# Gated-linear heads of a hybrid block: tanh swishes, late squares, and low parts of weight tiles made by VectorE instead of GpSimd

## The chip, the cores and the metric

One core of a Trainium2 chip runs the whole kernel as one program. The metric is the device time of that core in microseconds. Three runs before the change took 5358.28, 5361.36 and 5364.64 us; the median is 5361.36.

## The reference

The reference is one layer: a normalised input is projected by one large matrix; a state-space branch (SSD), a gated linear branch (HGRN2) and gates are mixed and projected; then follows a mixture of experts over product keys. Sequence 512, width 2048, all in float32. The change touches the gated linear branch alone (16 heads, key and value width 128):

```
qh = silu(hq);  f = lb + (1 - lb) * sigmoid(hf);  kh = 1 - f;  log_f = log(f);  vh = hi
per chunk:  bcum = cumsum(log_f)
            scores[t,s] = sum_k q[t,k] k[s,k] exp(bcum[t,k] - bcum[s,k])      (s <= t)
            o = scores @ v + (q * exp(bcum)) @ state
            state = exp(b_end) * state + (k * exp(b_end - bcum))^T @ v
o = rms(o) * hg_norm_w * silu(hg);   y_hg = o
```

`hq`, `hf`, `hi`, `hg` are the projections of the normalised input `h` (512 x 2048) with the head's columns of four 2048 x 2048 matrices. `rms(o)` is `o * rsqrt(mean(o^2) + 1e-6)` over the head's 128 values.

## The kernel before

**Stages.** `program` runs stages one after the other: norm, SSD, the gated heads (`hg_stage`, L726, from 798.5 us to about 1827 us of the profiled execution), two mix stages, an output projection, and the experts. Channels lie on the partitions and the 512 tokens on the free axis.

**A product in float32.** Each weight tile (128 output channels, 128 x 2048 numbers in SBUF) is split in two rounded parts: `high` is a rounded copy made by ScalarE (`split_high`, L148), `low = raw - high` is made by GpSimd (`split_low`, L155). `product` (L168) adds for each of 16 steps three matmuls of 128x128 by 128x512: high by h_high, high by h_low, low by h_high; 48 matmuls a tile, 24 in each half of a tile. The ring `Ring` has two slots each of `raw`, `high` and `low`. SP loads raw tile n when the low part of tile n-2 is done (`load_tile`, L127: one 1 MB transfer). ScalarE makes the high part of tile n when TensorE has used tile n-2 and the load has landed. `ring.used` counts the tiles that TensorE has finished.

**A head.** Four tiles, in the order f, q, v (hi), g (hg); n = 4u + s is tile s of head u. The accumulators `acc[0]` and `acc[1]` alternate; each is free for its next tile when what was in it has been read (`acc_read`). The computation on head p = u - 1 is placed by TensorE between the halves of head u's tiles:

- `turn` (L871): four transposes each of v and of the decayed keys `lev[:, L8]`, into `ps_v` and `ps_k`.
- `part_a` (L879, L880): for one chunk c of 128 tokens, seven level products and one for the diagonal, into `ps_lev`. It needs the preceding block to have been read (`a_read`).
- `part_b` (L889 to L894): for chunk c the value product, for c > 0 the product with the state, for c < 3 the new state's contribution. It needs `probs` of the chunk and, for c > 0, the state.
- after the first half of tile 3, the sum of squares over the head's channels with a matrix of ones (L928).

**VectorE** (in the order of its queue, for u in the loop): copies v_tok and k_tok from PSUM; `take_probs(p, 0)` and `(p, 1)` (a masked product L995 and a sum over levels L997); `take_f(u)`: sigmoid of f by an addition, a reciprocal (L971) and a scaling, then k = 1 - f, and four scans of the logarithms (L979); `next_state` and `take_probs` for chunks 0 to 3; the swish of q: `1 + exp(-x)` (L986), reciprocal (L987), multiply (L988); `exponents(u)`: differences for seven levels in halves (L1017, L1018) and two more rows, with `next_state(p, 2)` among them; the copy of v out of its accumulator (L1064); `weigh(u)`: 14 multiplies (L1029, L1030), copies, `qe`, the copy of four columns `k_end` (L1036) and the decayed keys (L1037); then `o_norm` of head p in two operations (L1073 with the root, L1075 with the gate); the swish of g like that of q.

**ScalarE**: high part of tile 1; exp of -f; Ln of f; high part of tile 2; exp of -q; high part of tile 3; one exponential of nine level rows (L844, 4608 columns, after all differences); squares of the output (L847, after `part_b` of chunk 3); high part of the next head's tile 0; Ln and Exp for the inverse root (L851, L853); exp of -g. All functions are in one set of activation tables, loaded once in this stage.

**Order around the change.** There is no planner: each engine runs its own queue in the written order with semaphore waits. The head loop runs over u = 1..15 with a first body (projection only) and a last one (computation only) outside of it. SP stores o_norm of head u - 2 after the four loads of head u.

Of the kernel before, what the change touches and what calls it, by code (L numbers as in the profile page):

```python
# [27 lines left out]
EXP_LN_SET = "natural_log_exp_and_others"  # L28

P = 128  # L30
# [695 lines left out]
def hg_stage(nc, dram, ring, h, const, y_out, following):  # L726
# [8 lines left out]
    with ExitStack() as ctx:  # L735
# [7 lines left out]
        norm_w = sb("norm_w", [P, 1])  # L743
        f = sb("f", [P, T])
# [28 lines left out]
        f_exp, q_exp, g_exp, f_ready, f_log, b_ready = (  # L773
            sem(n) for n in ("f_exp", "q_exp", "g_exp", "f_ready", "f_log", "b_ready"))
# [4 lines left out]
        lev_ready = sem("lev_ready")  # L779
        a_done = sem("a_done")  # L780
# [4 lines left out]
        squared, summed, rooted = sem("squared"), sem("summed"), sem("rooted")  # L785
        o_ready = sem("o_ready")
        o_stored = sem("o_stored")
        act_done, vec_done = sem("act_done"), sem("vec_done")
        block = ctx.enter_context(nc.Block())

        @block.sync
        def _(sp):
# [10 lines left out]
            for s in range(HG_TILES):  # L803
                load_tile(sp, ring, s % 2, dram["w_hg"][HG_TILES + s], HG_TILES + s)
            with sp.Fori(2, H) as u:
# [3 lines left out]
                store(u - 2)  # L809
            load_ahead(sp, ring, H * HG_TILES, following)  # L810
            store(H - 2)
            store(H - 1)
            sp.wait_ge(o_stored, 16 + 16 * H)

        @block.gpsimd
        def _(pool):
            split_low_all(nc, pool, ring, H * HG_TILES)

        @block.scalar
        def _(act):  # L820
# [5 lines left out]
            def body(u, proj, comp):  # L826
                p = u - 1
                for s in range(HG_TILES):
                    n = HG_TILES * u + s
                    if proj:  # L830
                        split_high(nc, act, ring, (s + 1) % 2, n + 1, 2 * u + (s + 1) // 2)
                    if s == 0 and proj:
                        act.wait_ge(ring.used, ring.base + n + 3)
                        act.wait_ge(lev_ready, u + 1)
                        nc.scalar.activation(f[:], acc[0][:], ACT.Exp, scale=-1.0).then_inc(f_exp, 1)
                        act.wait_ge(f_ready, u + 1)
                        nc.scalar.activation(b[:], f[:], ACT.Ln).then_inc(f_log, 1)
                    if s == 1 and proj:
                        act.wait_ge(ring.used, ring.base + n + 3)
                        nc.scalar.activation(sg[:], acc[1][:], ACT.Exp, scale=-1.0).then_inc(q_exp, 1)  # L840
                    if s == 2:
                        if proj:
                            act.wait_ge(lev_diff, u + 1)
                            nc.scalar.activation(lev[:, 0:LK], lev[:, 0:LK], ACT.Exp).then_inc(lev_exp, 1)  # L844
                        if comp:
                            act.wait_ge(b_done, NC * p + NC)
                            nc.scalar.activation(o_sq[:], ps_o[:], ACT.Square).then_inc(squared, 1)  # L847
                    if s == 3:
                        if comp:
                            act.wait_ge(summed, p + 1)  # L850
                            chain.after(nc.scalar.activation(rstd[:], ps_k[:], ACT.Ln, bias=const["eps"],  # L851
                                                             scale=1.0 / P))
                            nc.scalar.activation(rstd[:], rstd[:], ACT.Exp, scale=-0.5).then_inc(rooted, 1)  # L853
                        if proj:
# [5 lines left out]
            with act.Fori(1, H) as u:  # L860
                chain.enter(u - 1, 1)
                body(u, True, True)
# [1209 lines left out]
```

## Time and profile before

| | value |
|---|---|
| median of three runs | 5361.36 us |
| profiled execution, its time | 5372.8 us |
| its span | 5370.8 us |
| mean granted TensorE clock | 0.963 |
| TensorE matmuls, busy | 4992.5 us, 93% |
| VectorE, busy | 3406.7 us, 63% |
| ScalarE, busy | 1451.5 us, 27% |
| GpSimd, busy | 2024.3 us, 38% |

"Busy" is the sum of the times in which an engine's instructions ran, and "span" goes from the first instruction to the last. The granted clock is the share of 2.4 GHz that TensorE was given: 0.5 is 1.2 GHz. Consecutive matmuls overlap in these records, so that the distance from one start to the next (the pitch) is what a matmul costs in a stream; a matmul of 512 columns lasts 0.39 us but starts some 0.23 us after the one before. The same holds to a lesser degree for VectorE and ScalarE.

### The profile page before, as it was taken

How to read it: one execution, taken by the hardware profiler on the slowest of the kernel's cores; microseconds unless marked ns; L12 is line 12 of the kernel's file. 1: busy time of each engine (PE TensorE's matmuls, PEld its weight loads, DVE VectorE, ACT ScalarE, POOL GpSimd, SP SyncE). 2: the span in 40 equal slices, each digit the busy share in tenths (PEclk: the TensorE clock that was granted, in tenths of full speed). 3: DMA queues.
4: the chain of work that ended last, by engine and by line, in shares of the span. 5: the costliest groups of instructions: out<-in, count | busy, mean ns of one | idle time of the engine just before them, and what ended most of it. 6: DMA issues, size and time to landing. Idle time of an engine off the chain costs nothing. (4 is left out here: it accounts for less than half of the span.)

```text
span 5370.8 us, 69570 instructions
## 1 busy us (share of the span) xinstructions
PE 4992.5 (93%) x25836; PEld 4479.2 (83%) x25836; DVE 3406.7 (63%) x4674; ACT 1451.5 (27%) x1170; POOL 2024.3 (38%) x624
## 2 busy tenths in 40 slices
PE   6999979999889899999869989999999799999997
PEld 5877857777777688788658989999999799999997
DVE  3566657888888500100127879998444588888886
ACT  2233222222222222211222324343222222222222
POOL 2333313333333244344334445556989411111111
PEclk7999989999999899999989999999999899999999
DMA  2222212121122223333323337777877888888884
GB/s 76 87 86 86 82 53 75 67 81 67 66 70 80 84 105 107 143 117 117 147 98 108 115 132 278 257 263 281 304 298 298 314 300 300 299 301 300 300 300 159
DMA packets 230889, 913.26 MB, mean 170 GB/s; under 512 B 18353, under 2 KB 100913, under 8 KB 152625
## 3 DMA queue, kind: packets, MB, share of 16 engines
q1 hardware_dynamic: 193968, 644.12, 34.6%
q0 software_dynamic: 36864, 268.45, 13.4%
q8 instruction: 29, 0.48, 0.0%
q14 instruction: 28, 0.22, 0.0%
HBM read 837.00 MB, written 75.50 MB: 170 GB/s over the span
## 5 line engine op out<-in xcount | busy, mean ns | idle before, releaser
L157 POOL TENSOR_TENSOR ring_low<-ring_raw,ring_high 128x2048 fp32r<-128x2048 f32 x337 | 1648.3, 4893 | 2068.9 <-ACT ring_high L152 2068.2
L175 PE MATMUL rt_acc<-h_high,ring_high 128*128 128x384 f32 (+1 forms) x2304 | 793.7, 345 | 24.5 <-POOL ring_low L157 21.5
L176 PE MATMUL rt_acc<-h_low,ring_high 128*128 128x384 f32 (+1 forms) x2304 | 785.9, 341 | 0.0
L177 PE MATMUL rt_acc<-h_high,ring_low 128*128 128x384 f32 (+1 forms) x2304 | 785.8, 341 | 0.0
L152 ACT ACTIVATE ring_high<-ring_raw 128x2048 fp32r<-128x2048 f32 x337 | 645.0, 1914 | 390.3 <-PE out_acc L177 125.1
L1695 DVE CUSTOM_DVE_ANT_0 sb_rt_rows<-sb_rt_rows,sb_rt_h_tok 128x2048 f32<-128x2048 f32 x128 | 339.4, 2651 | 277.7 <-DMA sb_rt_rows<-u_rows,row_of 274.5
L175 PE MATMUL hg_acc<-h_high,ring_high 128*128 128x512 f32 x1024 | 429.2, 419 | 59.8 <-POOL ring_low L157 50.5
L1319 POOL DMA_INDIRECT sb_op_rows<-v_tiles,row_of x128 | 122.6, 958 | 948.0 <-DVE sb_op_total L1860 922.5
L175 PEld LDWEIGHTS rt_acc<-h_high,ring_high 128*128 128x128 f32 x2304 | 433.9, 188 | 41.2 <-POOL ring_low L157 17.0
L176 PEld LDWEIGHTS rt_acc<-h_low,ring_high 128*128 128x128 f32 x2304 | 433.9, 188 | 10.0
L177 PEld LDWEIGHTS rt_acc<-h_high,ring_low 128*128 128x128 f32 x2304 | 433.5, 188 | 10.3
L176 PE MATMUL hg_acc<-h_low,ring_high 128*128 128x512 f32 x1024 | 410.3, 401 | 0.0
L177 PE MATMUL hg_acc<-h_high,ring_low 128*128 128x512 f32 x1024 | 410.2, 401 | 0.0
L1833 PE MATMUL op_out<-sb_op_w_high,ring_high 128*128 128x384 f32 x1024 | 343.3, 335 | 26.6 <-DVE sb_op_w_low L1876 26.6
L1833 PE MATMUL op_out<-sb_op_w_high,sb_op_more_high 128*128 128x384 f32 x1024 | 343.4, 335 | 7.2 <-DVE sb_op_more_low L1866 7.2
L1835 PE MATMUL op_out<-sb_op_w_high,sb_op_more_low 128*128 128x384 f32 x1024 | 343.2, 335 | 0.0
L1834 PE MATMUL op_out<-sb_op_w_low,sb_op_more_high 128*128 128x384 f32 x1024 | 343.1, 335 | 0.0
L1834 PE MATMUL op_out<-sb_op_w_low,ring_high 128*128 128x384 f32 x1024 | 343.0, 335 | 0.0
L1835 PE MATMUL op_out<-sb_op_w_high,ring_low 128*128 128x384 f32 x1024 | 343.0, 335 | 0.0
L175 PE MATMUL ssd_acc<-h_high,ring_high 128*128 128x512 f32 x768 | 304.3, 396 | 0.0
L1896 DVE TENSOR_TENSOR x_mid_back<-x_mid_back,op_out 128x384 f32<-128x384 f32 x512 | 270.2, 548 | 49.9 <-PE op_out L1835 49.9
L1860 DVE SCALAR_TENSOR_TENSOR sb_op_total<-sb_op_rows,own_weight,sb_op_total 128x2048 f32<-128x2048 f32 x128 | 300.1, 2345 | 0.0
(294 smaller groups left out, 10031.0 us busy)
## 6 DMA issues: line engine op xcount, KB each, us to landing
ring_raw<-u_tiles SPq DMA_DIRECT2D x128, 1024.0 KB, 5.1
ring_raw<-v_tiles SPq DMA_DIRECT2D x128, 1024.0 KB, 6.0
ring_raw<-w_hg SPq DMA_DIRECT2D x64, 1024.0 KB, 4.8
ring_raw<-w_ssd SPq DMA_DIRECT2D x48, 1024.0 KB, 4.8
ring_raw<-w_mix_s SPq DMA_DIRECT2D x32, 1024.0 KB, 4.8
ring_raw<-w_mix_h SPq DMA_DIRECT2D x32, 1024.0 KB, 4.9
gelu<-sb_rt_gelu SPq DMA_DIRECT2D x128, 192.0 KB, 4.9
gates<-sb_rt_table SPq DMA_DIRECT2D x12, 2048.0 KB, 8.4
```

The lines of the kernel that those rows point to most:

```text
L152: nc.scalar.activation(ring.high[:, slot], ring.raw[:, slot], ACT.Copy).then_inc(ring.high_ready, 1)
L157: nc.gpsimd.tensor_tensor(ring.low[:, slot], ring.raw[:, slot], ring.high[:, slot].bitcast(F32), ALU.subtract).then_inc(ring.low_ready, 1)
L175: nc.tensor.matmul(out, high[:, m], x_high[:, k, tokens], start=(k == 0), stop=False, skip_group_check=True)
L176: nc.tensor.matmul(out, high[:, m], x_low[:, k, tokens], start=False, stop=False, skip_group_check=True)
L177: last = nc.tensor.matmul(out, low[:, m], x_high[:, k, tokens], start=False, stop=(k == KT - 1), skip_group_check=True)
L1319: return pool.indirect_dma_start(rows[0:OWN, slot], None, table, bass.IndirectOffsetOnAxis(ap=row_of[0:OWN, k:k + 1], axis=0))
L1695: vec.tensor_tensor_reduce(rows[0:OWN, slot], rows[0:OWN, slot], h_tok[0:OWN], 1.0, 0.0, ALU.mult, ALU.add, dot[0:OWN, slot:slot + 1]).the ...
L1833: nc.tensor.matmul(o, v_high[s][:, m], w_high[:, buf, j], start=(j == 0), stop=False)
L1834: nc.tensor.matmul(o, v_high[s][:, m], w_low[:, buf, j], start=False, stop=False)
L1835: last = nc.tensor.matmul(o, v_low[s][:, m], w_high[:, buf, j], start=False, stop=(j == GROUP - 1))
L1860: vec.scalar_tensor_tensor(total[0:OWN], rows[0:OWN, slot], weight[0:OWN, ds(k, 1)], total[0:OWN], ALU.mult, ALU.add).then_inc(summed, 1)
L1896: vec.tensor_tensor(x, x, ps_out[d][:, 0:REST], ALU.add).then_inc(out_added, 1)
```

## The change

It keeps the mathematics of the heads and changes who does what, and when:

- **Late squares.** The sum of squares of head p goes to TensorE's slot after the first half of tile 0 of the head after next; the root and the last multiply (now a factor in `ps_k`) follow there. Before that `o_norm` receives `ps_o * norm_w * og` (`o_weighed`). The loop has a third part, `fin`, for head u - 2, and runs over u = 2..15 with two bodies ahead of it and two behind.
- **Low parts.** VectorE makes all four low parts of a head at fixed places of its queue (`low(u, s)`). GpSimd has no instruction in this stage.
- **Order of TensorE.** The computation moves ahead by about half a tile: `part_a` and `part_b` end after the second half of tile 2, and both halves of tile 3 run without an interruption. `turn(ps_k, ...)` moves behind the second half of tile 0.
- **Order of VectorE and ScalarE.** `take_f` comes ahead of `k_tok` and `take_probs(p, 1)`; `exponents` ahead of `take_probs(p, 3)`; v is read after `weigh`. The exponential of the level rows is cut in two (five rows and four), and `k_end` is copied by ScalarE.
- **SP.** Stores stand after the second load of a head, for head u - 3.

The core of the diff (unchanged lines of the moved parts left out):

```diff
+                nc.scalar.preload_act_table_set(EXP_LN_SET)
+                if proj:
+                    next_high(0)
+                if fin:
+                    act.wait_ge(summed, e + 1)
+                    chain.after(nc.scalar.activation(rstd[:], ps_k[:], ACT.Ln, bias=eps4[:], scale=1.0 / P))
+                    nc.scalar.activation(ps_k[:], rstd[:], ACT.Exp, scale=-0.5).then_inc(rooted, 1)
+                if proj:
+                    act.wait_ge(ring.used, ring.base + HG_TILES * u + 3)
+                    act.wait_ge(lev_ready, u + 1)
+                    nc.scalar.activation(f[:], acc[0][:], ACT.Exp, scale=-1.0).then_inc(f_exp, 1)
+                    next_high(1)
+                    act.wait_ge(f_ready, u + 1)
+                    nc.scalar.activation(b[:], f[:], ACT.Ln).then_inc(f_log, 1)
+                    nc.scalar.preload_act_table_set(EXP_TANH_SET)
+                    act.wait_ge(ring.used, ring.base + HG_TILES * u + 4)
+                    nc.scalar.activation(sg[:], acc[1][:], ACT.Tanh, scale=0.5).then_inc(q_tanh, 1)
+                    next_high(2)
+                    act.wait_ge(lev_diff, 2 * u + 1)
+                    nc.scalar.activation(lev[:, 0:FIRST_EXP], lev[:, 0:FIRST_EXP], ACT.Exp).then_inc(lev_exp, 1)
+                    act.wait_ge(lev_diff, 2 * u + 2)
+                    nc.scalar.activation(lev[:, FIRST_EXP:LK], lev[:, FIRST_EXP:LK], ACT.Exp).then_inc(lev_exp, 1)
+                    act.wait_ge(lev_exp, 2 * u + 2)
+                    if comp:
+                        act.wait_ge(state_ready, (NC - 1) * p + (NC - 1))
+                    nc.scalar.activation(k_end[:], ..., ACT.Copy).then_inc(k_end_ready, 1)
+                if comp:
+                    act.wait_ge(b_done, NC * p + NC)
+                    nc.scalar.activation(o_sq[:], ps_o[:], ACT.Square).then_inc(squared, 1)
+                if proj:
+                    next_high(3)
+                    act.wait_ge(ring.used, ring.base + HG_TILES * u + 6)
+                    act.wait_ge(acc_read, HG_TILES * u + 4)
+                    nc.scalar.activation(sg[:], acc[1][:], ACT.Tanh, scale=0.5).then_inc(g_tanh, 1)
...
+                half(0, 0)
+                if fin:
+                    pe.wait_ge(squared, e + 1)
+                    nc.tensor.matmul(ps_k[:], const["ones"], o_sq[:], start=True, stop=True).then_inc(summed, 1)
+                if comp:
+                    pe.wait_ge(lev_ready, p + 2)
+                    pe.wait_ge(acc_read, HG_TILES * p + 5)
+                    turn(ps_v, v)
+                    part_a(p, 0)
+                half(0, 1)
+                if comp:
+                    pe.wait_ge(o_ready, p + 1)
+                    turn(ps_k, lev[:, L8])
+                    part_a(p, 1)
+                half(1, 0)
+                if comp:
+                    part_b(p, 0)
+                    part_a(p, 2)
+                half(1, 1)
+                if comp:
+                    part_b(p, 1)
+                    part_a(p, 3)
+                half(2, 0)
+                if comp:
+                    part_b(p, 2)
+                half(2, 1)
+                if comp:
+                    part_b(p, 3)
+                half(3, 0)
+                half(3, 1)
...
+            def low(u, s):
+                slot, n = s % 2, HG_TILES * u + s
+                dve.wait_ge(ring.high_ready, ring.base + n + 1)
+                vec.tensor_tensor(ring.low[:, slot], ring.raw[:, slot], ring.high[:, slot].bitcast(F32),
+                                  ALU.subtract).then_inc(ring.low_ready, 1)
...
+            def twice_swish(dst, src, tanh_done, value, taken):
+                dve.wait_ge(tanh_done, value)
+                vec.scalar_tensor_tensor(dst[:], sg[:], 1.0, src[:], ALU.add, ALU.mult).then_inc(acc_read, 1)
+                dve.wait_ge(acc_read, taken)
...
             def weigh(u, p, comp):
-                dve.wait_ge(lev_exp, u + 1)
                 for l, w in enumerate(HALVES):
+                    if l == 0:
+                        dve.wait_ge(lev_exp, 2 * u + 1)
+                    if l == FIRST_EXP:
+                        dve.wait_ge(lev_exp, 2 * u + 2)
+                        low(u, 4)
...
+                if proj:
+                    low(u, 1)
                 if comp:
                     dve.wait_ge(turned, 2 * p + 1)
                     vec.tensor_copy(v_tok[:].rearrange("p c v -> p (c v)"), ps_v[:]).then_inc(turned_read, 1)
+                if fin:
+                    dve.wait_ge(rooted, e + 1)
+                    dve.wait_ge(o_weighed, e + 2)
+                    vec.tensor_tensor(o_norm[:], o_norm[:], ps_k[:], ALU.mult).then_inc(o_ready, 1)
+                if comp:
+                    take_probs(p, 0)
+                if proj:
+                    take_f(u)
+                if comp:
                     dve.wait_ge(turned, 2 * p + 2)
                     vec.tensor_copy(k_tok[:].rearrange("p c v -> p (c v)"), ps_k[:]).then_inc(turned_read, 1)
                     take_probs(p, 1)
                 if proj:
+                    low(u, 2)
+                    sum_logs(u)
                 if comp:
                     next_state(p, 0)
                     take_probs(p, 2)
                     next_state(p, 1)
+                if proj:
+                    twice_swish(q, acc[1], q_tanh, u + 1, n + 4)
+                    low(u, 3)
+                    if comp:
+                        dve.wait_ge(a_done, NC * p + NC)
+                    exponents(u)
+                if comp:
                     take_probs(p, 3)
                     next_state(p, 2)
                 if proj:
                     weigh(u, p, comp)
                     dve.wait_ge(ring.used, ring.base + n + 5)
                     vec.tensor_copy(v[:], acc[0][:]).then_inc(acc_read, 1)
+                    dve.wait_ge(acc_read, n + 5)
                 if comp:
+                    dve.wait_ge(squared, p + 1)
                     dve.wait_ge(o_stored, 16 * p + 16)
+                    if fin:
+                        dve.wait_ge(o_ready, e + 2)
+                    vec.scalar_tensor_tensor(o_norm[:], ps_o[:], norm_w[:, 0:1], og[:],
+                                             ALU.mult, ALU.mult).then_inc(o_weighed, 1)
+                    dve.wait_ge(o_weighed, p + 2)
                 if proj:
+                    twice_swish(og, acc[1], g_tanh, u + 1, n + 6)
```

`next_high(s)` is `split_high` of tile s + 1 of the head. `sum_logs` is the part of `take_f` with the scans.

## Rows read from the trace of the kernel before

**Rows 1.** Stretches: us, busy time of each engine, granted clock, DMA share, GB/s.

```profile
900.00:1780.00 880.00, 800.00 (x3988) 668.32 (x3987) 741.71 (x903) 213.98 (x168) 313.68 (x56) 0.96 0.20 71
300.00:700.00 400.00, 395.15 (x1946) 318.33 (x1945) 261.20 (x326) 118.15 (x125) 137.00 (x31) 1.00 0.24 85
```

**Rows 2.** Waits of TensorE, 850 to 1795 us: total, times, longest.

```profile
PE hg_acc L175 <- POOL ring_low L157: 49.1, 14, 3.5
PE hg_ps_k L928 <- ACT sb_hg_o_sq L847: 33.1, 15, 2.2
```

**Rows 3.** TensorE in order of time, one head: start, us, line [idle before].

```profile
1229.59 0.79 PE L175 MATMUL hg_acc<-h_high,ring_high 128*128 128x512 f32 x1 [3.50 <-POOL ring_low L157]
...
1236.69 0.60 PE L871 MATMUL hg_ps_v<-c_ident,sb_hg_v 128*128 128x128 f32 x4
...
1244.82 1.72 PE L879 MATMUL hg_ps_lev<-sb_hg_lev 128*128 128x128 f32 x14
...
1246.52 0.48 PE L175 MATMUL hg_acc<-h_high,ring_high 128*128 128x512 f32 x1
...
1252.10 0.39 PE L889 MATMUL hg_ps_o<-sb_hg_probs,sb_hg_v_tok 128*128 128x128 f32 x2
...
1254.25 0.48 PE L175 MATMUL hg_acc<-h_high,ring_high 128*128 128x512 f32 x1
...
1279.54 0.39 PE L177 MATMUL hg_acc<-h_high,ring_low 128*128 128x512 f32 x1
1282.13 1.12 PE L928 MATMUL hg_ps_k<-sb_hg_o_sq,c_ones 128*128 128x512 f32 x2 [2.20 <-ACT sb_hg_o_sq L847]
...
1292.22 0.79 PE L175 MATMUL hg_acc<-h_high,ring_high 128*128 128x512 f32 x1 [3.48 <-POOL ring_low L157]
```

**Rows 4.** Groups of the stage: busy us, mean ns; the last: ns min/median/max, starts.

```profile
L997 DVE TENSOR_REDUCE sb_hg_probs<-sb_hg_masked 128x128 f32<-128x1024 f32 x64 | 128.0, 2000 | 2.2
L987 DVE RECIPROCAL sb_hg_sg<-sb_hg_sg 128x512 f32<-128x512 f32 x32 | 107.3, 3353 | 1.1
L995 DVE TENSOR_TENSOR sb_hg_masked<-hg_ps_lev,sb_hg_mask 128x1024 f32<-128x1024 f32 x64 | 78.0, 1219 | 64.8 <-PE hg_ps_lev L880 64.8
...
L152 ACT ACTIVATE ring_high<-ring_raw 128x2048 fp32r<-128x2048 f32 x64 | 121.8, 1903 | 0.0
L844 ACT ACTIVATE sb_hg_lev<-sb_hg_lev 128x4608 f32<-128x4608 f32 x16 | 64.8, 4052 | 237.4 <-DVE sb_hg_lev L1021 237.4
...
L157 POOL TENSOR_TENSOR ring_low<-ring_raw,ring_high x64: 4574/4632/8132, 805.2 to 1789.1; 128x2048 fp32r<-128x2048 f32 x64
```

**Rows 5.** Three lines by instance: ns min/median/max, first and last start.

```profile
L1036 DVE COPY sb_hg_k_end<-sb_hg_lev x16: 4495/4506/4516, 849.9 to 1792.8; 128x4 f32<-128x4 f32 x16
...
L1075 DVE TENSOR_TENSOR sb_hg_o_norm<-sb_hg_o_norm,sb_hg_og x16: 691/4058/4083, 914.8 to 1826.3; 128x512 f32<-128x512 f32 x16
...
L1866 DVE TENSOR_TENSOR ring_low<-ring_raw,ring_high x63: 2227/2286/2293, 4238.0 to 5285.1; 128x2048 fp32r<-128x2048 f32 x63
```

**Rows 6.** VectorE in order of time, same head.

```profile
1249.96 0.42 DVE L968 TENSOR_SCALAR sb_hg_sg<-sb_hg_f 128x512 f32<-128x512 f32 x1
...
1254.53 0.43 DVE L975 TENSOR_SCALAR sb_hg_k<-sb_hg_f 128x512 f32<-128x512 f32 x1
1255.26 1.37 DVE L979 TENSOR_TENSOR_SCAN sb_hg_b<-c_ones,sb_hg_b 128x128 f32<-128x128 f32 x4 [0.30 <-ACT sb_hg_b L837]
...
1271.53 0.42 DVE L1017 TENSOR_TENSOR sb_hg_lev<-sb_hg_b 128x256 f32<-128x256 f32 x1
...
1276.49 0.42 DVE L1019 COPY sb_hg_lev<-sb_hg_b 128x512 f32<-128x512 f32 x1
```

**Rows 7.** ScalarE in order of time, a table switch of the earlier stage.

```profile
519.69 1.28 ACT L436 ACT_TABLE_LOAD   x1
520.99 0.69 ACT L436 ACTIVATE sb_ssd_rstd<-ssd_ps_decay,c_eps 128x512 f32<-128x512 f32 x1
```

**Rows 8.** One matmul of each step, whole stage: ns min/median/max, first and last start.

```profile
L175 PE MATMUL hg_acc<-h_high,ring_high x1024: 387/389/798, 798.8 to 1793.0; 128*128 128x512 f32 x171
```

More of the change, by code:

```diff
@@ L28 @@
 EXP_LN_SET = "natural_log_exp_and_others"
+EXP_TANH_SET = "exp_and_others"
 P = 128
@@ L801, in store @@
                 sp.dma_start(one(y_out[ds(p, 1)]), o_norm[:]).then_inc(o_stored, 16)
-            for s in range(HG_TILES):
-                load_tile(sp, ring, s % 2, dram["w_hg"][HG_TILES + s], HG_TILES + s)
-            with sp.Fori(2, H) as u:
+            for n in range(HG_TILES, 3 * HG_TILES):
+                load_tile(sp, ring, n % 2, dram["w_hg"][n], n)
+            with sp.Fori(3, H) as u:
                 for s in range(HG_TILES):
@@ L808, in _ @@
                     load_tile(sp, ring, s % 2, one(dram["w_hg"][ds(n, 1)]), n)
-                store(u - 2)
+                    if s == 1:
+                        store(u - 3)
             load_ahead(sp, ring, H * HG_TILES, following)
-            store(H - 2)
-            store(H - 1)
+            for p in range(H - 3, H):
+                store(p)
             sp.wait_ge(o_stored, 16 + 16 * H)
-        @block.gpsimd
-        def _(pool):
-            split_low_all(nc, pool, ring, H * HG_TILES)
         @block.scalar
@@ L824, in _, with body, next_high @@
             nc.scalar.activation(lb_in[:], lb_in[:], ACT.Exp).then_inc(lb_step, 1)
-            def body(u, proj, comp):
-                p = u - 1
-                for s in range(HG_TILES):
+            def body(u, proj, comp, fin):
+                p, e = u - 1, u - 2
+                def next_high(s):
                     n = HG_TILES * u + s
[L830 to L854, printed above, removed]
-                            act.wait_ge(ring.used, ring.base + n + 3)
-                            act.wait_ge(acc_read, HG_TILES * u + 4)
-                            nc.scalar.activation(sg[:], acc[1][:], ACT.Exp, scale=-1.0).then_inc(g_exp, 1)
@@ new lines, in body @@
+                if proj:
[16 more added lines that the diff above has]
+                        act.wait_ge(state_ready, (NC - 1) * p + (NC - 1))
+                    nc.scalar.activation(k_end[:], lev[:, L7].rearrange("p (c t) -> p c t", c=NC)[:, :, CH - 1],
+                                         ACT.Copy).then_inc(k_end_ready, 1)
@@ L866, in _ @@
+            body(1, True, True, False)
+            with act.Fori(2, H) as u:
+                chain.enter(u - 2, 1)
+                body(u, True, True, True)
+            chain.leave(H - 2)
+            body(H, False, True, True)
+            body(H + 1, False, False, True)
         @block.tensor
@@ L895, in part_b, with body, half @@
                 last.then_inc(b_done, 1)
[L897 to L899 removed]
+            def body(u, proj, comp, fin):
+                p, e = u - 1, u - 2
+                def half(s, i):
                     n = HG_TILES * u + s
[L902 to L937 removed]
@@ L939, in _ @@
-            body(0, True, False)
-            with pe.Fori(1, H) as u:
-                body(u, True, True)
-            body(H, False, True)
+                    if not proj:
+                        return
+                    if i == 0:
+                        pe.wait_ge(ring.low_ready, ring.base + n + 1)
+                        pe.wait_ge(acc_read, n + 1)
+                    last = product(nc, acc[s % 2][:], ring.high[:, s % 2], ring.low[:, s % 2], h[0], h[1],
+                                   range(i * KT // 2, (i + 1) * KT // 2))
@@ L944, in _ @@
+                half(2, 1)
[3 more added lines that the diff above has]
+                half(3, 1)
+            body(0, True, False, False)
+            body(1, True, True, False)
+            with pe.Fori(2, H) as u:
+                body(u, True, True, True)
+            body(H, False, True, True)
+            body(H + 1, False, False, True)
         @block.vector
```

129 lines of the change are left out of this document (39 added, 90 removed).

## The prediction

> **What bounds the kernel now.** I read the busy shares, then the stage in stretches, then who waits, then TensorE and VectorE in order of time. In the steady heads TensorE is busy 800.0 of 880 us at a granted clock of 0.96, VectorE 741.7; the 400 us of the earlier stage show 395.2 of 400 at 1.00 [rows 1]. So TensorE's stream is the floor, and about a tenth of it is lost. The list of waits gives two losses, 14 and 15 times: 3.5 us for `ring_low` and 2.2 us for the squares [rows 2]. The timeline shows a third: the first half tile of a head takes 1236.69 - 1229.59 = 7.10 us after the 3.50 us wait, while the one that ends the stretch from 1246.52 to 1252.10 takes 5.58; the first matmul after the wait lasts 0.79 us, where one before the squares lasts 0.39: half the granted clock (1.2 of 2.4 GHz), then the full one [rows 3]. One head takes 1292.22 - 1229.59 = 62.63 us.
>
> Without the losses a head is: a first half of 5.55, then 1236.69 to the end of the sixth later interruption, 1279.54 + 0.23 = 1279.77, 43.08 us, then 0.56 for the sum over squares (half of the row's 1.12, whose two records overlap like all here) and the last half of 5.55: **54.7 us** [rows 3]. The parts I need: both transposes and the first level block 2.57 (from 1236.69 to the half that ends at 1244.82, so began at 1239.26), a level block 1.70 (1244.82 to 1246.52), first value product with the third level block 2.15 (1252.10 to 1254.25). The remaining small work in 43.08, less six halves of 5.55 and 2.57 + 1.70 + 2.15, is 3.4: about 2.4, 0.6 and 0.4.
>
> GpSimd takes 4.6 us for a low part where nothing disturbs it, up to 8.1 [rows 4]. Why it is late: its operand waits for ScalarE's high part, and that stands in ScalarE's queue behind the 4.05 us exponential of all nine level rows, which waits for VectorE. VectorE in turn carries two reciprocals of 3.35 us for swishes [rows 4], a 4.5 us copy of 128x4 and an o_norm multiply of 4.06 us whose shortest instance is 0.69 [rows 5]: I read nearly all of both as VectorE held off while GpSimd is on a low part.
>
> **The change, part by part, per head.** VectorE's own sum: two reciprocals and their additions go (2 x 3.35, and 0.43 each by the row at 1249.96 for the same shape), -7.6; the k_end copy goes to ScalarE, -4.5; the multiply falls from 4.06 to 0.69, -3.4; four low parts come, 4 x 2.29 [rows 5], +9.2. Net about -6.3 from 741.7 / 880 x 62.7 = 52.8 us: 46.5. It stays under 54.7. GpSimd's 4.6 us and more per tile leave the path; the wait for the low part of the next head's first tile goes if VectorE gives it in time.
>
> That is a matter of order, so I lay it out. Zero is TensorE's start on a head. TensorE with the new order: half to 5.5, sum 6.1, turn v and level block 0 to 8.3, half to 13.8, turn k and block 1 to 15.9, half to 21.5, value product 0 and block 2 to 23.6, half to 29.2, product 1 and block 3 to 31.6, half to 37.2, product 2 37.8, half to 43.3, product 3 43.7, two halves to 54.7.
>
> VectorE starts its long run when the f tile is done: 13.8, ScalarE's exponential 0.6 and two hand-overs of 0.1 to 0.3, so 14.8. The row at 1249.96 to the one at 1254.53 is 4.57 [rows 6]: k starts at 19.3. k 0.4, k_tok 0.6: 20.3. Block 1's masked product 1.2 (21.5) and sum 1.95: 23.5. Low part 2 at a pitch of 2.2: 25.7. Four scans 1.3: 27.0. State 0.2, block 2's probabilities 3.2, state 0.3: 30.7. The q swish 0.75, 31.4. Low part 3 must wait for ScalarE: q's tile ends at 29.2, tanh, then the high part of 1.90 [rows 4] to 31.9: so 31.9 to 34.2. Level differences: 1276.49 - 1271.53 = 4.96 less one state update of 0.26 = 4.7 [rows 6], two more operations about 1.0: 39.9. Probabilities 3: 43.0. State: 43.3. TensorE wants these at 43.3 for product 3. **That is a tie**, the tightest place; the masked product of block 1, read at 21.5, stands against block 2 at 21.95, and that of block 2 at 28.5 against block 3 at 29.9.
>
> From 43.3: ten weighings at 0.335, 46.7 (their exponentials, 4.05 x 5/9 = 2.3 from 37.6 and 1.9 from 39.9, are done by 41.8). Low part 4: ScalarE copies k_end after the last state, squares after product 3 (43.9 to 44.5), high part to 46.4; low 46.7 to 48.9, wanted at 54.7. Four weighings, four copies and products: 52.1; v read from its bank at 52.8, which TensorE wants at 54.7: 1.9 spare. The og swish waits for the last tile and ends at 56.4, 1.7 into the next head.
>
> Next head: ScalarE's tanh ends at 0.9, table load 1.28 [rows 7], high part to 4.1; low part 1 at 4.1 to 6.4, wanted at 15.9. The squares are a head old, so the 2.2 us wait goes; Ln and Exp to 7.6, o_norm 8.6, probabilities 0 to 11.8, and VectorE idles until 14.8. The gap takes up all late work of the loop turn. The transfers: a slot is loaded when VectorE's low part frees it (6.4, 25.7, 34.2, 48.9) and its high part is wanted 8 us later or more, against some 5 us that a tile took; SP's store now stands after the second load and waits for an o_norm written 25 us before. Hidden.
>
> The two table switches cost 1.28 each in the row, with the next activation 0.02 later [rows 7]. The Trainium skill (ScalarE: Activation LUTs, What ACT_TABLE_LOAD costs) gives 1.28 plus a drain, 2.66 in all, and its advice to group functions by set speaks against switching twice a head. With its price low part 1 would end at 7.8 and probabilities 0 at 13.2: still inside the idle gap, so the sum would differ only in the tail, by 1.4 us.
>
> **The sum.** Before, TensorE's projections run from 798.8 to 1793.0 + 0.7: 994.9 us [rows 8]. After: head 0 has no computing beside it: 192 matmuls at 0.227 (5.45 / 24, a half less its first 0.1) = 43.5 and 1.8 for the cold start; then 15 heads of 54.7 plus 0.4, taken for loop turns and for the tie at product 3, the side the estimates err to: 15 x 55.1 = 826.5. 871.8 in all: 123 saved. Tail: before 33.3 us from the last projection to the last o_norm at 1826.3 + 0.7 [rows 5, 8], which includes waiting for the k_end copy and two reciprocals; with these gone, four probabilities at 3.2, hand-overs, one root and one multiply make about 25: 8 saved, bounds 4 and 12 (the two reciprocals alone, and all the k_end and multiply waiting besides). Together 131. The profiled execution took 5372.8 (span 5370.8): it would be 5242. The median of the runs is 11.4 lower than the profiled one; the same saving gives **5230 us**.
>
> Unseen prices: a tanh of 128x512, bounded by the exponentials of the shape at 0.60 and 0.63; ScalarE's output into PSUM, never in these rows, between 0 and 1 us more than the 0.63 into SBUF, and inside the idle gap; the scalar_tensor_tensor of a swish, 0.69 to 0.75 by the multiply of the shape. The low part on VectorE is taken at 2.29; from above GpSimd's longest, 8.13 [rows 4]. The row of 2.29 is nearest: the same form on the same tiles, 63 times; below it lies its own shortest, 2.23.
>
> **Rivals.**
> 1. VectorE's run sets the pace at product 3. It is tied, so each microsecond too little in my run from 14.8 to 43.3 (some twenty operations and six hand-overs) is a microsecond of TensorE's idle time per head. For 1 to 3 us: 15 to 45 us given back, 5245 to 5275; I take 5260. For: no slack at all. Against: pitches are from this stage, some taken under GpSimd's disturbance.
> 2. The same wait grows past 3 us, and the clock falls as behind the 3.5 us wait, at least 1.6 us more (1229.59 to 1236.69 against 5.55). Head 59 to 61: saving 131 - 15 x 5 = 55: 5305.
> 3. Slower: a low part costs on VectorE what it cost disturbed on GpSimd, say 6.4, the middle of 4.63 and 8.13 [rows 4], because the tiles' memory and not the engine sets its pace while loads and ScalarE use it. Two lie in the run before product 3: +8.2, and +2 for the clock (1.6 and rounding): a head of 64.9, 15 x 64.9 + 45.3 = 1018.8 against 994.9, less the tail's 8: 5377. It decides from a low part of about 5.8. Against it: none of 63 over 2.293 with loads running [rows 5].
> 4. No effect: TensorE finds a new wait of equal size in each head, such as turn k behind o_ready (8.6 against 13.8, 5 us spare; it must be 13 late): 5361.
>
> **Chances.** Forecast 0.6, rival 1 0.22, rival 2 0.08, rival 3 0.06, rival 4 0.04. The forecast's own width is 5222 (no friction, tail 12) to 5245; the range, 5220 to 5285, takes rival 1 whole. A measurement of this kernel tells 0.2%, 11 us, from no change: faster 0.9, same 0.04, slower 0.06.
>
> **What would show it.** Stage: last projection near 1671; granted clock 1.00 in the steady heads, TensorE idle under 1 us a head. VectorE: low parts at 2.29 with ScalarE's high part as releaser at low parts 1 and 3 alone; the longest idle time before the f addition, about 3 us; no 4 us instance of the o_norm multiply; 46 us busy a head. TensorE's wait, if any, at product 3. If instead waits stand at block 2 or at the first half of a head, my order of VectorE's work is wrong; if the clock is below 0.98 with no waits above 2 us, the floor is.

## The result, and the profile after

The changed kernel takes **5236.4 us** (median of four runs, 5234.6 to 5238.1) against 5363.0 us before; the ratio is 0.9757, 95% interval 0.9745 to 0.9768. Forecast: 5230, range 5220 to 5285. The profiled execution went from 5372.8 to 5234.9 us. 137.9 us are more than the 126.6 of the medians because the profiled execution of before lay 9.8 above its median, that of after 1.5 below.

Stretches of the changed kernel (columns as in [rows 1]): the steady heads, and the tail behind the last projection. In the first TensorE is busy without a gap at the full clock, where [rows 1] had 800 of 880 us at 0.96; GpSimd did nothing.

```profile
900.00:1640.00 740.00, 740.00 (x3863) 627.83 (x3862) 606.31 (x846) 251.42 (x217) 0.00 (x0) 1.00 0.23 80
...
1669.10:1691.70 22.60, 14.45 (x97) 11.40 (x95) 17.10 (x17) 6.34 (x8) 0.00 (x0) 0.94 0.03 12
```

The row of the first matmul of each step, and those of the low part and the late o_norm multiply (ns min/median/max, first and last start). The first answers to [rows 8]: 868.2 us between the first and the last start, against 994.2. The second is [rows 5]'s price for a low part; the third has no instance near the 4 us of before.

```profile
L176 PE MATMUL hg_acc<-h_high,ring_high x1024: 387/389/767, 800.2 to 1668.4; 128*128 128x512 f32 x171
...
L990 DVE TENSOR_TENSOR ring_low<-ring_raw,ring_high x64: 2278/2292/2297, 808.4 to 1660.9; 128x2048 fp32r<-128x2048 f32 x64
...
L1082 DVE TENSOR_TENSOR sb_hg_o_norm<-sb_hg_o_norm,hg_ps_k x16: 686/687/689, 908.1 to 1691.0; 128x512 f32<-128x512 f32 x16
```

The list of waits between 850 and 1668 us holds no line of TensorE; both of [rows 2] are gone. VectorE waits for ScalarE's high part twice a head and for f's exponential once:

```profile
DVE ring_low L990 <- ACT ring_high L153: 46.3, 30, 2.5
DVE sb_hg_sg L996 <- ACT sb_hg_f L845: 43.7, 15, 2.9
```

VectorE in order of time, the head whose first matmul starts at 1229.7 (1235.16, where the sum of squares starts, less a half of 5.45). To be seen: the gap of 2.92 before the f gate, the 0.59 before low part 3, and the state that is done at 1272.80 + 0.35.

```profile
1233.86 2.29 DVE L990 TENSOR_TENSOR ring_low<-ring_raw,ring_high 128x2048 fp32r<-128x2048 f32 x1 [2.46 <-ACT ring_high L153]
...
1244.61 0.43 DVE L996 TENSOR_SCALAR sb_hg_sg<-sb_hg_f 128x512 f32<-128x512 f32 x1 [2.92 <-ACT sb_hg_f L845]
...
1261.79 2.29 DVE L990 TENSOR_TENSOR ring_low<-ring_raw,ring_high 128x2048 fp32r<-128x2048 f32 x1 [0.59 <-ACT ring_high L153]
...
1270.88 2.01 DVE L1024 TENSOR_REDUCE sb_hg_probs<-sb_hg_masked 128x128 f32<-128x1024 f32 x1
1272.80 0.35 DVE L1032 SCALAR_TENSOR_TENSOR sb_hg_state<-sb_hg_state,sb_hg_k_end,hg_ps_state 128x128 f32<-128x128 f32 x1
...
1281.95 0.69 DVE L1110 COPY sb_hg_v<-hg_acc 128x512 f32<-128x512 f32 x1
```

TensorE's product 3 of the same head starts 0.1 us behind that state. Its first matmul needs only the probabilities, whose sum over levels ended at 1270.88 + 2.01 = 1272.89; the matmul that reads the state is the second:

```profile
1273.26 0.38 PE L903 MATMUL hg_ps_o<-sb_hg_probs,sb_hg_v_tok 128*128 128x128 f32 x2
1273.48 0.39 PE L906 MATMUL hg_ps_o<-sb_hg_qe,sb_hg_state 128*128 128x128 f32 x2
```

### The profile page after: what moved, and what is told of

The parts are those of the page before. It is cut to its first block and busy times, and to the rows that moved or that the text cites. A ratio compares the mean times of both kernels' runs of the same rounds, so it can differ in the third digit from the quotient of the medians.

```text
span 5232.2 us, 69516 instructions
## 1 busy us (share of the span) xinstructions
PE 4945.5 (95%) x25836; PEld 4450.6 (85%) x25836; DVE 3275.9 (63%) x4660; ACT 1503.2 (29%) x1236; POOL 1661.0 (32%) x560
## 5 line engine op out<-in xcount | busy, mean ns | idle before, releaser
L158 POOL TENSOR_TENSOR ring_low<-ring_raw,ring_high 128x2048 fp32r<-128x2048 f32 x273 | 1294.9, 4744 | 2295.7 <-ACT ring_high L153 2295.0
L176 PE MATMUL hg_acc<-h_high,ring_high 128*128 128x512 f32 x1024 | 408.4, 399 | 9.2 <-DVEq L968 9.2
L178 PE MATMUL ssd_acc<-h_high,ring_low 128*128 128x512 f32 x768 | 300.3, 391 | 0.0
```

The costliest lines, as they stand in the source:

```text
L158: nc.gpsimd.tensor_tensor(ring.low[:, slot], ring.raw[:, slot], ring.high[:, slot].bitcast(F32), ALU.subtract).then_inc(ring.low_ready, 1)
L176: nc.tensor.matmul(out, high[:, m], x_high[:, k, tokens], start=(k == 0), stop=False, skip_group_check=True)
L178: last = nc.tensor.matmul(out, low[:, m], x_high[:, k, tokens], start=False, stop=(k == KT - 1), skip_group_check=True)
```

## The experiments

"Stage" below is the distance between the first and the last start of the projections' first matmul, in the profiled execution: 994.2 before, 868.2 after. I compare by it because one later stage, the experts' routing, took 1378 to 1383 us in some executions and 1408 to 1413 in others, whichever of these kernels ran; the medians of whole runs carry that 30 us.

| | median, us | stage, us | one head, us | TensorE's waits in the stage, us a head |
|---|---|---|---|---|
| before | 5363 to 5368 | 994.2 | 62.6 or 63.7 | low part 3.5, squares 2.2 |
| after | 5236.4 | 868.2 | 54.9 | none |
| e1 low parts on GpSimd | 5296.5 | 930.4 | 59.0 | product 3 1.7, k_tok 1.1, block 2 0.4 |
| e2 tanh alone | 5261.6 | 893.4 | 56.6 | low part 1.4 |
| e3 VectorE low parts alone | 5307.4 | 935.4 | 58.6 or 60.2 | squares 2.2, state 0.7 |
| e4 exp swishes | 5287.6 | 918.0 | 58.0 | product 3 2.8; v's bank 2.2 once |
| e5 one operation in the run | 5240.8 | 875.1 | 55.4 | product 3 0.2 |
| e6 four operations | 5282.5 | 914.1 | 57.5 or 59.0 | product 3 2.3 |
| e7 two behind product 3 | 5237.7 | 868.7 | 54.9 | none |
| e8 sum back in tile 3 | 5223.2 | 870.5 | 55.0 | none |
| e9 idle work on GpSimd | 5322.5 | 958.3 | 59.2 or 60.8 | product 3 2.8, block 2 0.4; v's bank 7.7 once |
| e10 two switches in the gap | 5239.6 | 868.4 | 54.9 | none |
| e11 two switches in the run | 5285.1 | 917.5 | 57.35 or 58.9 | product 3 2.1; v's bank 1.9 once |
| e12 five behind product 3 | 5239.6 | 898.8 | 56.8 | v's bank 1.6 |

"One head" is the distance between two f gates (`sb_hg_sg<-sb_hg_f` on VectorE) once the loop runs steadily. Where two lengths stand, the longer head has a stretch at half the clock (before the change both have one, the longer head a longer one). "Once" is a wait at the start of head 1, ahead of the steady heads.

**What carries the gain.** e1 takes the low parts back to GpSimd:

```diff
             def low(u, s):
-                ... (wait and subtraction)
+                return
+        @block.gpsimd
+        def _(pool):
+            split_low_all(nc, pool, ring, H * HG_TILES)
```

> The changed kernel with one part undone: GpSimd makes the four low parts of a head again, VectorE makes none. Theory A (order and tanh carry the gain; the low parts on VectorE carry nothing of it): TensorE's stream of 54.9 us a head stays the bound, GpSimd's 4.6 us ends before each tile is wanted, time within 0.3% of the changed kernel, 5236 us. Theory B (VectorE and GpSimd hold each other off, so the low parts had to move): copies and tensor_scalar operations of VectorE wait 2 to 4 us again in the run from f to product 3 and TensorE waits there, 2 to 5 us a head: 5265 to 5310 us.

Measured: 62 us more stage. My theory A fell, B's figures held. The result of the low part is never late in the steady heads (no wait for `ring_low` behind 850 us). VectorE has less to do than in the changed kernel, 578.1 us busy in 800 against 606.3 in 740, 42.6 us a head against 45.0, and is late all the same, because its own work is held off: of the fourteen level differences the first now takes 4.85 us, started 0.04 behind GpSimd's low part, and f's scaling 2.75 where it took 0.55. The sum of eight stretches of 100 us from 900 us on, then VectorE, then GpSimd in this kernel:

```profile
sum 800.00, PE 756.24 PEld 630.89 DVE 578.11 ACT 251.25 POOL 296.32; mean PE 94.53 PEld 78.86 DVE 72.26 ACT 31.41 POOL 37.04
```

```profile
1233.94 4.85 DVE L1043 TENSOR_TENSOR sb_hg_lev<-sb_hg_b 128x256 f32<-128x256 f32 x1 [0.90 <-DVE sb_hg_q L1016]
...
1277.67 2.75 DVE L1000 TENSOR_SCALAR sb_hg_f<-sb_hg_sg,sb_hg_lb 128x512 f32<-128x512 f32 x1 [0.19 <-DVE sb_hg_sg L999]
```

```profile
1233.90 4.60 POOL L158 TENSOR_TENSOR ring_low<-ring_raw,ring_high 128x2048 fp32r<-128x2048 f32 x1 [12.81 <-ACT ring_high L153]
1250.48 7.99 POOL L158 TENSOR_TENSOR ring_low<-ring_raw,ring_high 128x2048 fp32r<-128x2048 f32 x1 [11.98 <-ACT ring_high L153]
...
1275.51 4.62 POOL L158 TENSOR_TENSOR ring_low<-ring_raw,ring_high 128x2048 fp32r<-128x2048 f32 x1 [8.07 <-ACT ring_high L153]
```

The Trainium skill (SBUF — State Buffer, Who interferes with whom) says that the two engines share one pair of ports under an exclusive lock, that a VectorE instruction with two SBUF inputs contends there with a GpSimd instruction that reads SBUF, and that the order of issue decides which of them blocks the other. These rows agree: the difference that starts at 1233.94 ends at 1238.79, 0.29 behind the end of GpSimd's low part (1233.90 + 4.60), f's scaling, started at 1277.67, ends 0.29 behind another (1275.51 + 4.62), and GpSimd's 4.6 becomes 8 at 1250.48, in the middle of VectorE's weighings.

e9 tests that alone: all as after, and GpSimd subtracts constants that nobody reads. The core of its edit:

```diff
...
+                pool.wait_ge(ring.high_ready, i + (ring.base + 2))
+                for j in range(2):
+                    nc.gpsimd.tensor_tensor(pool_spare[:, j], mask[:], mask[:], ALU.subtract)
```

> The changed kernel, VectorE still making the low parts, with idle work on GpSimd beside it: at each high part it subtracts two constant tiles of 128x1024 into a spare tile, twice, about 4.6 us in all, which nobody waits for. Theory B (the two engines hold each other off on their common way to SBUF): VectorE's low parts and the first operation behind them last up to 4.6 us longer, the run to product 3 grows by 2.3 to 7 us and TensorE waits there: stage 35 to 120 us longer. Rival (GpSimd's work costs VectorE nothing; what made the kernel with low parts on GpSimd slower was waiting for the results alone): under 5 us.

Measured: 90 us more, inside B's range; 10 of them fall once, before the steady heads, where TensorE waits 7.7 us for v's copy. In a steady head two level differences of 2.12 and 2.11 us stand in a row, each behind one of GpSimd's two operations; low part 3 itself kept 2.29, against the expectation. The rival is out, since nobody waits for GpSimd's results here:

```profile
1248.57 2.29 DVE L1001 TENSOR_TENSOR ring_low<-ring_raw,ring_high 128x2048 fp32r<-128x2048 f32 x1 [0.45 <-ACT ring_high L153]
1250.78 2.12 DVE L1053 TENSOR_TENSOR sb_hg_lev<-sb_hg_b 128x256 f32<-128x256 f32 x1
1252.82 2.11 DVE L1054 TENSOR_TENSOR sb_hg_lev<-sb_hg_b 128x256 f32<-128x256 f32 x1
```

e2 is the kernel before with the tanh swishes only (norm weight halved, 4 eps, four switches a head):

```diff
-                chain.after(vec.tensor_scalar(sg[:], sg[:], 1.0, None, ALU.add))
-                chain.after(vec.reciprocal(sg[:], sg[:]))
-                vec.tensor_tensor(dst[:], src[:], sg[:], ALU.mult).then_inc(acc_read, 1)
+                vec.scalar_tensor_tensor(dst[:], sg[:], 1.0, src[:], ALU.add, ALU.mult).then_inc(acc_read, 1)
```

> The kernel before with one part of the change: both swishes by tanh (four table switches a head), all else in the old order, low parts on GpSimd. Theory A: the level differences end 5.1 us earlier, so the exponential ends near 46.8 us into a head of 62.6 and not 52, the squares are ready before TensorE asks, and the low part of the next head's first tile is late by 0 to 1.2 us only: head 55 to 56.5, saving 90 to 115 us, 5250 to 5275 us. Theory B: GpSimd's low part is still the last thing at the head's end, disturbed to 6 to 8 us, and the 3.5 us wait stays while only the wait for the squares goes: head near 60, saving 35 to 45 us, 5320 us.

Measured: 100.8 of the stage's 126.0 us, a head of 56.6 us, so theory A. The squares' wait is gone and one for GpSimd is left (14 instances, 1.4 us each); one low part of that kernel, at 1235.34, lasts 8.17 us:

```profile
PE hg_acc L176 <- POOL ring_low L158: 18.9, 14, 1.4
```

e3 is the other part alone, `low(u, s)` at the start, behind `take_f`, behind the q swish and after ten weighings:

```diff
-            split_low_all(nc, pool, ring, H * HG_TILES)
...
+                    low(u, 1)
...
+                    low(u, 2)
...
+                    low(u, 3)
...
+                    low(u, 4)
```

> The kernel before with the other part alone: VectorE makes the low parts (tile 1 at the head's start, 2 behind the f gate, 3 behind the q swish, 4 behind ten weighings), swishes by reciprocals, old order. Both theories: k_end's copy falls from 4.5 to under 0.3 us and every o_norm multiply to 0.7 us, since GpSimd is idle. Theory A (the level run to the squares is what counts): 4.4 us more in that run, TensorE's wait for the squares grows from 2.2 to about 6.6 us and eats what the vanished 3.5 us wait gives: 5345 to 5400 us, no gain. Theory B (the mutual holding off is what cost): several us less on VectorE in each head, time 5270 to 5310 us.

Measured: 58.8 us off the stage. k_end's copy and the o_norm multiply fell as both theories said, below; A was wrong on the time. The run from the scans to the last level difference went from 1255.26 to 1276.83 + 0.68 before ([rows 6] for its start) to 1227.40 to 1250.93 here: 22.3 to 23.5 us, though two low parts of 2.2 us were put in. Of the 3.2 us that they did not cost, 2.7 had been in it already: a wait of 1.44 us for TensorE's block 3 and an addition (L986) that took 1.72 and not 0.43 behind GpSimd. VectorE of the kernel before, then two groups of e3:

```profile
1262.46 1.23 DVE L995 TENSOR_TENSOR sb_hg_masked<-hg_ps_lev,sb_hg_mask 128x1024 f32<-128x1024 f32 x1 [1.44 <-PE hg_ps_lev L880]
...
1265.67 1.72 DVE L986 TENSOR_SCALAR sb_hg_sg<-sb_hg_sg 128x512 f32<-128x512 f32 x1
...
1276.83 0.68 DVE L1021 TENSOR_TENSOR sb_hg_lev<-sb_hg_b 128x512 f32<-128x512 f32 x1
```

```profile
L1040 DVE COPY sb_hg_k_end<-sb_hg_lev x16: 158/162/164, 849.0 to 1735.5; 128x4 f32<-128x4 f32 x16
...
L1083 DVE TENSOR_TENSOR sb_hg_o_norm<-sb_hg_o_norm,sb_hg_og x16: 692/692/694, 908.3 to 1764.6; 128x512 f32<-128x512 f32 x16
```

So neither part is enough, and the two overlap: 100.8 and 58.8 alone, 126.0 with both and the new order. The new order does not pay by itself. With the tanh swishes and GpSimd's low parts, the new order and what goes with it give a stage of 930.4 (e1), the old order 893.4 (e2): 37 us worse. In e1 f's scaling and the first level difference, both in the run to product 3, stand where GpSimd is on a low part. With VectorE's low parts and the old swishes the new order is 17 us better (e4 918.0, e3 935.4). The 62 us of e1 are thus the price of GpSimd's low parts in this order, not in general. Both parts in the old order were not run, so the order's own share of the 126.0 is open. e4 is the changed kernel with the old swishes and no switches:

```diff
-                vec.scalar_tensor_tensor(dst[:], sg[:], 1.0, src[:], ALU.add, ALU.mult).then_inc(acc_read, 1)
+                chain.after(vec.tensor_scalar(sg[:], sg[:], 1.0, None, ALU.add))
+                chain.after(vec.reciprocal(sg[:], sg[:]))
+                vec.tensor_tensor(dst[:], src[:], sg[:], ALU.mult).then_inc(acc_read, 1)
```

> The changed kernel with its swishes by exp, addition and reciprocal again (no table switches then), new order, low parts on VectorE. Theory A (product 3 is tied to VectorE's run): the q swish adds 3.8 us of which 0.5 lay in the wait for low part 3: TensorE waits 3.2 us at product 3, plus up to 2.4 us of half clock behind it: 15 x 3.2 to 5.6 = 48 to 84 us slower, 5285 to 5320 us. Rival (there is slack in the order that the layout misses): under 15 us slower.

Measured: 49.8 us: 3.06 in each steady head (57.98 against 54.92) and 4.0 once before them; the wait at product 3 is there in all 15 heads, 2.8 us each, and the stretches from 900 to 1700 us all show a granted clock of 1.00.

```profile
PE hg_ps_o L901 <- DVE sb_hg_probs L1023: 41.7, 15, 2.8
```

e8 puts the sum of squares back to tile 3 (`half(3, 0)`, sum, `half(3, 1)`).

```diff
-                if fin:
-                    pe.wait_ge(squared, e + 1)
-                    nc.tensor.matmul(ps_k[:], const["ones"], o_sq[:], ...).then_inc(summed, 1)
...
                 half(3, 0)
+                if comp:
+                    pe.wait_ge(squared, p + 1)
+                    nc.tensor.matmul(ps_k[:], const["ones"], o_sq[:], ...).then_inc(summed, 1)
                 half(3, 1)
```

> The changed kernel with TensorE's sum of squares back behind the first half of tile 3, where it was before the change; root and last multiply stay late. Theory A (the squares are ready 5 us before TensorE asks there, since the exponentials end early; their lateness is not what pays): no wait, stage within 2 us of the changed kernel. Rival (the late place is what removes the 2.2 us wait): 1 to 2.2 us a head, 15 to 33 us longer.

Measured: 2.3 us more stage, 0.09 a head, and no wait. TensorE asks at 1280.30 for squares that ScalarE began at 1275.00. The late place is not what removed the 2.2 us wait.

```profile
1275.00 0.60 ACT L864 ACTIVATE sb_hg_o_sq<-hg_ps_o 128x512 f32<-128x512 f32 x1 [0.50 <-PE hg_ps_o L906]
```

**How tight the order is.** e5, e6 and e7, e12 add operations of 0.7 us to VectorE: one and four ahead of `take_probs(p, 3)`, two and five behind `weigh`. That of e5:

```diff
+                    for _ in range(1): 
+                        chain.after(vec.tensor_tensor(spare[:], b[:], b[:], ALU.add))
```

> The changed kernel with one operation more on VectorE ahead of the probabilities of chunk 3 (the addition of two 128x512 tiles into a spare one, waited for: about 0.72 us), in each of 15 heads. Theory A (product 3 tied to VectorE's run, 0.1 us spare in the trace of the changed kernel): TensorE waits 0.6 us at product 3 in each head, stage 9 us longer. Rival (at least 1 us of slack there): no wait, stage unchanged within 1 us.

> The same with four such operations, 2.9 us. Theory A: a wait of 2.8 us at product 3 in each head, stage 42 us longer with the clock kept. Rival 2 of the prediction (the clock falls behind the wait): 1.6 us or more on top, stage 65 us or more longer. Slack theory: under 30 us.

> The changed kernel with two such operations, 1.4 us, behind the weighing and ahead of v's copy, past product 3. Theory A (2.0 us spare there): no wait on TensorE, stage unchanged within 2 us. Rival (VectorE's whole queue is the bound, every microsecond on it counts): 15 x 1.4 = 21 us longer.

> The changed kernel with five operations of 0.72 us, 3.6 us, ahead of v's copy, where the trace shows 2.0 us spare. Theory A: v is read 1.6 us after TensorE wants the accumulator, TensorE waits there at the head's first half: 15 x 1.6 = 24 us longer. If the two ops run had shown no cost for another reason than spare time, this one shows none either.

Measured: +6.9 and +45.9 us for 0.7 and 2.9 us in the run; +0.5 and +30.6 for 1.4 and 3.6 us behind it. A head of e5 takes 55.40 us, 0.48 more for 0.73 added; ten heads of e6 take 57.5, 2.57 more for 2.91, and five about 59.0, with a stretch at half the clock behind the wait: theory A, with the 1.5 us of rival 2 in a third of the heads. A head of e12 takes 56.77, 1.85 more for 3.6. Between the first and second pair lies the whole statement: some 0.3 us spare before product 3, 1.8 to 2.0 behind it. The wait of e12 is 24.6 us over 15 heads, 1.64 each (one of 2.84, the others 1.55), where 1.6 was expected:

```profile
PE hg_acc L176 <- DVE sb_hg_v L1113: 24.6, 15, 2.8
```

**The price of a table switch.** e10 puts two more at the head's start, e11 two between q's tanh and the next high part. That of e11:

```diff
+                    nc.scalar.preload_act_table_set(EXP_LN_SET)
+                    nc.scalar.preload_act_table_set(EXP_TANH_SET)
                     next_high(2)
```

> The changed kernel with two table switches more at the head's start (three in a row for one). Priced by the rows of the trace, 1.28 us each: the first high part ends 2.6 us later, inside VectorE's idle gap of 2.9 us before the f gate: no wait, stage within 3 us. A price of 2.66 us each, estimate by the Trainium skill (ScalarE: Activation LUTs, What ACT_TABLE_LOAD costs): 5.3 us later, the f gate starts 1.3 to 2.4 us late, and the tie at product 3 turns it into 15 to 35 us.

> The changed kernel with two table switches more between q's tanh and the high part of tile 3, which VectorE waits for in its run. By the rows, 2.6 us: low part 3 and so product 3 2.5 us later, stage 15 x 2.5 = 37 us longer. At 2.66 us a switch, estimate by the same page of the Trainium skill: 5.3 us later, 75 to 100 us longer with the clock. Slack theory: under 15 us.

Measured: +0.2 us in the gap; +49.3 in the run. ScalarE of e11: loads 1.29 apart, the high part 0.02 behind the last.

```profile
1282.07 1.28 ACT L852 ACT_TABLE_LOAD   x1
1283.36 1.28 ACT L853 ACT_TABLE_LOAD   x1
1284.66 1.92 ACT L153 ACTIVATE ring_high<-ring_raw 128x2048 fp32r<-128x2048 f32 x1
```

TensorE's product 3 in three heads of e11:

```profile
1007.75 0.38 PE L905 MATMUL hg_ps_o<-sb_hg_probs,sb_hg_v_tok 128*128 128x128 f32 x1 [2.14 <-DVE sb_hg_probs L1026]
...
1065.10 0.38 PE L905 MATMUL hg_ps_o<-sb_hg_probs,sb_hg_v_tok 128*128 128x128 f32 x1 [2.14 <-DVE sb_hg_probs L1026]
...
1124.06 0.38 PE L905 MATMUL hg_ps_o<-sb_hg_probs,sb_hg_v_tok 128*128 128x128 f32 x1 [2.15 <-DVE sb_hg_probs L1026]
```

A head is then 1065.10 - 1007.75 = 57.35 us, 2.43 over the 54.92 of the changed kernel: the two loads (2.57) less 0.14 that was to spare. In six of the 15 heads TensorE runs at half the clock right behind the wait; such a head takes about 58.9, like the one from 1065.10 to 1124.06. With 3.8 us once, at the wait of 1.9 us before the steady heads, that makes up the 49.3. The two heads above, and the 3.2 us behind the second wait:

```profile
1007.75:1065.10 57.35, 55.21 (x287) 46.54 (x287) 45.13 (x65) 21.29 (x18) 0.00 (x0) 1.00 0.23 78
1065.10:1124.06 58.96, 56.81 (x286) 47.74 (x287) 45.13 (x65) 21.28 (x18) 0.00 (x0) 0.97 0.23 76
1065.60:1068.80 3.20, 3.20 (x9) 2.53 (x9) 3.20 (x11) 2.40 (x2) 0.00 (x0) 0.50 0.00 0
```

The 2.66 us a switch of the Trainium skill (ScalarE: Activation LUTs, What ACT_TABLE_LOAD costs) would give 5.3 a head; the rows decide against it here.

## Why the prediction was right

- **The floor.** 54.7 us a head, taken as 55.1: from one tanh of g to the next are 54.92 (1229.99 to 1284.91, below), and all projections take 868.9 us (868.2 and one step), forecast 871.8. The term that carries nearly all of the gain came from TensorE's row of starts, not from the waits' sum; 3.5 + 2.2 alone would have missed the half clock and the time to restart. The head of 62.63 us that I read was the shorter of two kinds that alternate, 62.6 and 63.7; the sum took the whole stage from [rows 8] and so was not touched by it. ScalarE of the changed kernel:

```profile
1229.99 0.60 ACT L869 ACTIVATE sb_hg_sg<-hg_acc 128x512 f32<-128x512 f32 x1 [8.61 <-PE hg_acc L178]
...
1284.91 0.60 ACT L869 ACTIVATE sb_hg_sg<-hg_acc 128x512 f32<-128x512 f32 x1 [8.61 <-PE hg_acc L178]
```

- **The layout.** From the head's zero at 1229.7: f gate 14.9 (forecast 14.8), low part 3 at 32.1 (31.9), last state ready 43.45 (43.3), TensorE at product 3 43.56 (43.3), v read 52.9 (52.8), low part 1 from 4.2 (4.1). The tie was real and fell on the good side by some 0.3 us. That side was luck: the layout adds some twenty operations, most of them rounded to 0.1 us. e5 and e6 show the slope of rival 1, e12 the spare time behind.
- **The squares.** I put the end of the 2.2 us wait down to the late place of the sum. That was a wrong reason for a right term: with the tanh swishes the wait is gone in the old place and order (e2), and in the new order the old place costs 0.09 us a head (e8).
- **The tail.** 22.6 us against 33.3, 10.7 saved; forecast 8, bounds 4 to 12. I counted two reciprocals in the tail of before; there is one of 3.35, besides the 4.50 of the k_end copy, and behind the change there are two roots, not one. The half clock of TensorE before I left out: its granted clock was 0.74 in the tail (1793.7 to 1827.0) and is 0.94 now; a block of level products took 3.24 us there at the half clock and 1.83 at the full one. How much of the 10.7 each of these is was not separated. The tail of before, and its two blocks:

```profile
1793.70:1827.00 33.30, 18.43 (x95) 15.45 (x94) 25.83 (x22) 2.51 (x4) 3.52 (x1) 0.74 0.02 8
...
1806.70 3.24 PE L879 MATMUL hg_ps_lev<-sb_hg_lev 128*128 128x128 f32 x14 [3.56 <-DVE sb_hg_masked L995]
...
1811.48 1.83 PE L879 MATMUL hg_ps_lev<-sb_hg_lev 128*128 128x128 f32 x14 [0.87 <-DVE sb_hg_masked L995]
```

- **Rivals.** 2: the clock never fell in the heads of the changed kernel, but in e3, e6 and e11 it did in some heads behind waits of 2.1 to 2.3 us; I had set its onset at 3. 3: no low part over 2.297 us. 4: turn k finds o_ready done 5 us before.
- **VectorE's sum** came to 606.31 / 740 x 54.92 = 45.0 us a head, forecast 46.5. Most of the difference is one hold-off that I had not counted beside k_end and o_norm: the addition of the q swish, 1.72 us for 0.43, 1.3 a head. It did no harm in the forecast, whose layout held undisturbed prices.
- **Whole runs.** 131 forecast, 126.6 between medians, 136.7 in the stages of the two profiled executions (126.0 + 10.7). The executions scatter by about 10 us, so that much of the agreement is luck. Two slips in the working change nothing in the forecast: 131 - 15 x 5 is 56, not 55 (rival 2), and the lower end of the forecast's own width is 5220, not 5222.

The sum of squares' place and the advance of TensorE's computation by half a tile were not priced one by one; e8 shows the first to be worth nothing here. The order of the queues alone, without the two other parts, was not tried, nor were both parts in the old order.

## What to carry to other kernels

Where a tensor engine waits at two or three places of a loop, measure the stream without the waits (starts of rows, one loop turn) and lay the other engines' queues against it in one column: the sum of busy times says that they fit, the column says whether the one tight place does. A helper engine that is never waited for can still set the pace, by holding off a neighbour on the way to memory; look for one instruction of a line that lasts several times its shortest instance, and take the helper's work away or give it other hours. Moving a result later (the squares) is worth nothing if the same change makes it early enough. An order of the queues is laid out for one division of the work: with GpSimd's low parts the new order is 37 us slower than the old one (e1, e2), with VectorE's it is 17 us faster (e4, e3).

## What the runs showed of the hardware that I had not expected

- A VectorE `tensor_tensor` of 128x256 that starts within 0.1 us behind a GpSimd subtraction takes 4.85 us and not 0.42 (e1). It ends 0.29 us behind GpSimd's, so that the thirteen differences behind it meet no GpSimd work and take 0.41 to 0.42 each. GpSimd's next operation starts among the weighings and takes 8 us. The profile books both as duration, not as waiting.
- TensorE's granted clock fell from 2.4 to 1.2 GHz for some 3 us behind waits of 2.1 to 2.3 us in some heads and not in others of the same kernel (six of 15 in e3 and e11, five in e6), behind ten of the fifteen 2.8 us waits of e9, and behind none of the 2.8 us waits of e4. Such a head is 1.5 to 1.6 us longer. Which heads is open.
- An activation that writes PSUM (0.60) costs no more than one into SBUF (0.63).
- The routing stage has two lengths 30 us apart between executions of one kernel; its cause was not looked into.
